# All weights ahead of the experts in 1 MB units, high and low part in one slot

## The reference, cut to what matters

```python
h = rmsnorm(x)
proj = h @ w_in + b_in                  # 1024 -> q 512, k 128, v 128, xr 1024, yr 1024, gates 2048
attn = block_attention(rope(norm(q)), rope(norm(k)), v)        # 8 query heads, 2 key heads
xc = depthwise_conv(xr)                                        # 4 taps
lru = rglru(xc, forward) + rglru(xc, backward)                 # gates, decays, scan along tokens
rec = lru * gelu(yr)
merged = sigmoid(gA) * (attn @ w_attn_o) + sigmoid(gR) * (rec @ w_lru_o)
x = x + merged @ w_out
h = rmsnorm(x)
top_val, top_idx = top_k(h @ w_router + b_router, 4)           # 32 experts
x = x + sum over the 4 experts e of gate_e * (swiglu(h @ w_gu[e] + b_gu[e]) @ w_down[e] + b_down[e])
out = rmsnorm(x) * final_g
```

## Time and profile before

| what | us |
|---|---|
| runs | 1136.24, 1137.75, 1137.98; median 1137.75 |
| span of the profiled execution, first to last instruction | 1134.2 |
| what lies around the span, against the median of the runs | 3.55 |
| TensorE busy | 1084.8 |
| VectorE busy | 371.1 |
| ScalarE busy | 237.2 |
| DMA | 439.77 MB, 388 GB/s over the span |

### The profile page before, as it was taken

One profiled execution on the slowest core, in us unless ns is written; L12 is line 12 of the kernel. 1 busy time (PEld: TensorE's weight loads), 2 busy tenths in 40 slices (PEclk: granted clock), 3 DMA queues, 4 the chain that ended last, 5 costly groups with the idle time before them and its releaser, 6 DMA issues.

```text
span 1134.2 us, 12887 instructions
## 1 busy us (share of the span) xinstructions
PE 1084.8 (96%) x5407; PEld 503.4 (44%) x5407; DVE 371.1 (33%) x645; ACT 237.2 (21%) x369; POOL 2.6 (0%) x10
## 2 busy tenths in 40 slices
PE   7999999999999999999998989898989899899987
PEld 7999899633333333333333333333333333333332
DVE  6997887522212222122121211111211212121212
ACT  5399961211111111111111110011110101010102
POOL 0000000000000000000000000000000000000000
PEclk9999999899999999999999999999999999999999
DMA  9544277999999999999999999999999999999996
GB/s 353 185 178 149 84 287 300 419 425 399 431 425 428 426 434 432 433 426 435 431 429 436 430 430 436 429 430 436 430 432 433 429 436 430 427 427 429 426 428 247
DMA packets 25637, 439.77 MB, mean 388 GB/s; under 512 B 3425, under 2 KB 4065, under 8 KB 6273
## 3 DMA queue, kind: packets, MB, share of 16 engines
q1 hardware_dynamic: 24976, 438.27, 91.5%
q10 hardware_dynamic: 624, 0.99, 0.2%
HBM read 438.20 MB, written 1.05 MB: 387 GB/s over the span
## 4 chain that ended last, share of the span: by engine, by line
PE 67%; DMA 28%; DVE 2%; SPq 1%; ACT 1%; issue 0%; DVEq 0%
PE ps L1491 26%; DMA slots<-in_w_down_dram 22%; PE ps L1500 13%; PE ps L1172 13%; DMA slots<-in_w_gu_dram 5%; PE ps L1455 5%; PE ps L1436 3%; PE ps L1549 2%; DVE slots_r L725 1%; SPq L403 1%; PE ps L1229 1%; PE ps L1450 1%; PE ps L1414 1%; PE ps L1234 0%; PE ps L1526 0%; PE ps L1274 0%
## 5 line engine op out<-in xcount | busy, mean ns | idle before, releaser
L1500 PE MATMUL ps<-slots,lru 128*64 128x512 f32 x1024 | 239.8, 610 | 17.2 <-DMA slots<-in_w_down_dram 17.2
L1491 PE MATMUL ps<-slots,lru 128*64 128x512 f32 x1024 | 227.7, 594 | 11.7 <-DMA slots<-in_w_gu_dram 11.2
L1491 PE MATMUL ps<-slots,qT 128*64 128x512 f32 x984 | 223.8, 596 | 4.6 <-DMA slots<-in_w_gu_dram 4.6
L1491 PEld LDWEIGHTS ps<-slots,lru 128*64 128x64 f32 x1024 | 74.1, 137 | 160.8 <-issue 139.7
L1491 PEld LDWEIGHTS ps<-slots,qT 128*64 128x64 f32 x984 | 68.9, 137 | 152.2 <-issue 144.8
L1500 PEld LDWEIGHTS ps<-slots,lru 128*64 128x64 f32 x1024 | 68.5, 139 | 142.5 <-issue 123.5
L1100 DVE COPY lru<-ps 128x512 f32<-128x512 f32 x32 | 22.1, 692 | 322.9 <-PE ps L1491 322.9
L1172 PE MATMUL ps<-slots_r 128*128 128x256 f32 (+1 forms) x812 | 107.7, 291 | 0.2 <-DVE slots_r L725 0.2
L1172 PEld LDWEIGHTS ps<-slots_r 128*128 128x128 f32 x812 | 102.2, 191 | 5.4 <-issue 2.5
L653 ACT ACTIVATE lru<-ps 128x512 f32<-128x512 f32 x32 | 19.1, 598 | 395.3 <-PE ps L1491 395.3
L1082 DVE TENSOR_SCALAR lru<-sq,rank_col,small 128x64 f32<-128x64 f32 x64 | 17.2, 312 | 241.8 <-PE ps L1436 241.8
(11 more groups left out here) (200 smaller groups left out, 649.3 us busy)
## 6 DMA issues: line engine op xcount, KB each, us to landing
slots<-in_w_gu_dram SPq DMA_DIRECT2D x40, 4096.0 KB, 29.2
slots<-in_w_gu_dram SPq DMA_DIRECT2D x44, 2048.0 KB, 18.9
slots<-in_w_down_dram SPq DMA_DIRECT2D x20, 4096.0 KB, 28.4
slots<-in_w_down_dram SPq DMA_DIRECT2D x22, 2048.0 KB, 20.8
slots<-in_pre_dram SPq DMA_DIRECT2D x13, 2048.0 KB, 8.2
slots<-in_w_down_dram SPq DMA_DIRECT2D x8, 512.0 KB, 31.0
slots<-in_pre_dram SPq DMA_DIRECT2D x3, 1024.0 KB, 6.9
slots<-in_w_gu_dram SPq DMA_DIRECT2D x3, 1024.0 KB, 17.4
```

Of the source, the lines that this page charges most:

```text
L1491: ins = nc.tensor.matmul(ps[64 * side:64 * side + 64, 4 + b, :], xgT[i % 2][:, k, :], rows[r][:, o:o + BANK], start=(k == 0), stop=(k == K ...
L1500: ins = nc.tensor.matmul(ps[64 * side:64 * side + 64, bank, :], actT[(i - 1) % 2][:, k, :], w[:, r, side * BANK:(side + 1) * BANK], start= ...
```

## The change

All weights ahead of the experts are loaded in 29 units of 1 MB (half a chunk; k and v are one unit). A unit lies whole in the first half of a slot; its high part is written in the second half of the same slot and its low part over the whole. Units 0 to 5 take slots 5, 2, 3, 4, 0, 1, units 6 to 22 rotate through slots 5, 2, 3, 4, and later ones use slots 6 and 2 to 5. Of the input chunks a unit is 256 of 512 columns of each of the eight rows of a partition, so its source is in pieces of 1 KB; for chunks 0, 2 and 3 and the last five it is contiguous. Splits are per unit and have new places in the programs of ScalarE and VectorE. Slots 0 and 1 take the expert chunks 0 and 1 once q is done. The first half of wide takes chunk 7 instead of 3. TensorE does all eight branches, then the mix; the part of the mix that is done bank by bank has the last two blocks instead of four. The diff, cut to what is spoken of:

```diff
-        SLOT_ORDER = [2, 3, LOWS, SLOTS - 1, 0, 1, 4, 5]
-        EARLIER = [5, 0, 4, 0, 5, 0, 1, 1]
-        FREED = {2: [(branch_ps, 3)], 0: [(mixed_ps, 1)], LOWS: [(branch_ps, KD)], 4: [(mixed_ps, 2)]}
+        UNIT = CH // 2
+        UNITS = ([(c, h) for c in range(10) for h in range(1 if c == 3 else 2)]
+                 + [(10, 0), (10, 1), (11, 0), (11, 1), (13, 0), (13, 1), (12, 0), (12, 1), (14, 0), (14, 1)])
+        Q_UNIT, KV_UNIT, BR_UNIT, MIX_UNIT = 4, 6, 19, 25
+        UNIT_SLOT = [5, 2, 3, 4, 0, 1] + [2 + (u + 1) % 4 for u in range(6, 23)] + [LOWS, 2, 3, 4, 5, LOWS]
+        UNIT_FREED = {6: (group_done, 4), 7: (group_done, 4), 8: (group_done, 6), 9: (group_done, 8), 10: (qkv_done, 4),
+                      **{u: (group_done, 2 * u - 12) for u in range(11, 23)},
+                      23: (gate_ps, 32), 24: (branch_ps, 2), 25: (branch_ps, 3), 26: (branch_ps, 4), 27: (branch_ps, 6),
+                      28: (branch_ps, 7)}
+        SLOT_ORDER = [0, 1, 2, 3, 4, 5, LOWS, SLOTS - 1]
+        FREED = {0: (qkv_done, 2), 2: (branch_ps, KD), 3: (mixed_ps, 1), 4: (mixed_ps, 2), 5: (mixed_ps, 3),
+                 LOWS: (mixed_ps, 4)}
...
-        CAST_V = (5, 9)
+        CAST_V = (9, 10, 17, 18)
+        def unit_src(u):
+            c, h = UNITS[u]
+            if c in IN_CHUNK[1:]:
+                return pre[c].rearrange("p (k n) -> p k n", k=KD)[:, :, h * TOK:(h + 1) * TOK]
+            return pre[c, :, h * UNIT:(h + 1) * UNIT]
+        def unit_low(u):
+            return ring_r[UNIT_SLOT[u]][:, 0:UNIT]
+        def unit_high(u):
+            return ring_r[UNIT_SLOT[u]][:, UNIT:]
...
+            for u in range(4):
+                unit_load(u)
...
+            sp.dma_start(ring[LOWS][:, KD * TOK:], w_lru[0]).then_inc(lruw_in, 16)
+            for u in range(6, 11):
+                unit_load(u)
+            for k in range(2):
+                expert_load(k)
+            sp.wait_ge(gate_ps, 16)
+            sp.dma_start(ring[LOWS][:, KD * TOK:], w_lru[1]).then_inc(lruw_in, 16)
+            for u in range(11, 22):
+                unit_load(u)
+            sp.wait_ge(rec_ok, 2)
+            sp.wait_ge(pv_ps, NQ // 2)
             sp.dma_start(late[:, :], expert_src(n, j)).then_inc(extra_full[0], 16)
+            half_load(extra_rows(1, 0), EXTRA[1], 0, extra_full[1])
+            unit_load(22)
+            unit_load(23)
+            half_load(wide[:, 0:2048], 7, 0, slot_full[SLOTS - 1])
+            for u in range(24, 29):
+                unit_load(u)
+            expert_load(2)
+            half_load(wide[:, 2048:], 7, 1, slot_full[SLOTS - 1])
             sp.wait_ge(merged_ok, KD)
             half_load(extra_rows(1, 1), EXTRA[1], 1, extra_full[1])
+            for k in range(3, SLOTS - 1):
                 expert_load(k)
...
@@ ScalarE
-            split_high(4)
+            split_high(7)
+            split_high(8)
             lru_gates(0, range(4))
             act.wait_ge(qk_inv, 1)
             nc.scalar.activation(qk_rstd, qk_rstd, ACT.Sqrt).then_inc(qk_rs, 1)
-            split_high(6)
             for i in range(8, 14):
                 group(i)
                 if i == 9:
                     lru_decay(0, 0)
+                    split_high(11)
                 if i == 11:
                     lru_decay(0, 1)
                     lru_decay(0, 2)
             copy_qk()
             lru_root(0)
+            split_high(12)
             for i in range(14, 16):
                 group(i)
...
-            split_high(7)
+            split_high(13)
...
             lru_gates(1, [0])
-            split_high(8, [0])
+            split_high(14)
             pair_exps(0)
             lru_gates(1, [1])
             group_pair(16)
-            split_high(8, [1])
+            split_high(15)
...
             group_pair(18)
+            split_high(16)
             lru_decay(1, 0)
...
@@ VectorE
-            split_high(5)
-            split_low(5)
+            for u in (9, 10):
+                split_high(u)
+                split_low(u)
...
             lru_input(0)
-            split_low(6)
+            split_low(11)
             lru_square(0)
             lru_scaled(0)
+            split_low(12)
             lru_scan(0)
             lru_sum(0)
...
             lru_input(1)
-            split_high(9)
-            split_low(9)
+            split_low(16)
+            split_high(17)
+            split_low(17)
             pair_max(2)
...
             pair_attn(1)
+            split_high(18)
+            split_low(18)
             pair_max(3)
...
-            split_low(10)
+            split_low(19)
+            split_low(20)
             recurrent_low(1)
             attention_low()
-            split_low(11)
+            split_low(21)
             for g in range(KD):
...
-                if g == 1:
-                    split_low(12)
-                if g == 3:
-                    split_low(13)
-                if g == KD - 1:
-                    split_low_by_halves(14)
+                if g != 3:
+                    split_low(22 + g if g < 3 else 21 + g)
...
@@ TensorE
-            for g in range(4):
+            for g in range(KD):
                 branches(g)
-            mix(0)
-            for g in range(4, KD):
-                branches(g)
-            for c in range(1, 4):
+            for c in range(ENDS):
                 mix(c)
```

More of the change, by code:

```diff
@@ L513, in _ @@
             act.dma_start(sq[:, 1:, :], squares[:, 1:, :]).then_inc(sq_in, 16)
-            split_high(0)
-            split_high(1)
+            for u in range(4):
+                split_high(u)
             act.wait_ge(lam_e, 1)
@@ L753, in _ @@
             low_part(hT_lo, hT, hT_hi).then_inc(h_lo, 1)
-            split_low(0)
-            split_low(1)
+            for u in range(4):
+                split_low(u)
             dve.wait_ge(lam_e, 2)
@@ L1174, in product, with unit @@
                 return ins
-            def chunk(c, k):
-                return [b.rearrange("p (k n) -> p k n", k=k) for b in (high(c), low(c))]
+            def unit(u, k):
+                return [b.rearrange("p (k n) -> p k n", k=k) for b in (unit_high(u), unit_low(u))]
             def transposes(rows, tp0):
@@ L1202, in first_groups @@
             def first_groups():
-                w = chunk(0, KD)
+                w = [unit(u, 4) for u in range(2)]
                 for q, (a, b, ks) in enumerate(((0, 0, range(4)), (0, 0, range(4, KD)), (0, 1, range(KD)), (1, 0, range(KD)))):
                     if q < 2:
-                        pe.wait_ge(split_hi, q + 1)
+                        pe.wait_ge(*unit_high_ok(q))
                         pe.wait_ge(h_hi, q + 1)
@@ L1239, in _ @@
             for part in range(2):
-                chunk_in(Q_CHUNK + part)
-                w = chunk(Q_CHUNK + part, KD)
-                n_col = QW if part == 0 else 2 * KVW
+                pe.wait_ge(*unit_low_ok((Q_UNIT + 1, KV_UNIT)[part]))
+                w = [unit(Q_UNIT, 4), unit(Q_UNIT + 1, 4)] if part == 0 else [unit(KV_UNIT, KD)]
+                per, n_col = (4, QW) if part == 0 else (KD, 2 * KVW)
                 for t in range(T):
@@ L1245, in _ @@
                     product(ps[:, 2 * t + part, 0:n_col],
-                            [((hT_hi[:, k, toks], hT_lo[:, k, toks]), [b[:, k, :] for b in w]) for k in range(KD)]
+                            [((hT_hi[:, k, toks], hT_lo[:, k, toks]), [b[:, k % per, :] for b in w[k // per]])
+                             for k in range(KD)]
                             ).then_inc(qkv_done, 1)
@@ L1314, in _ @@
                     values(VALUES_AT.index(i))
-            BLOCKS = CH // P
-            w_br = [chunk(c, BLOCKS) for c in BR_CHUNK]
+            BLOCKS = UNIT // P
+            w_br = [unit(u, BLOCKS) for u in range(BR_UNIT, MIX_UNIT)]
             def branches(g):
                 first = 12 * g
-                for i, c in enumerate(BR_CHUNK[:2]):
-                    if g > 0 and first <= BLOCKS * i < first + 12:
-                        chunk_in(c)
                 if g >= 2:
@@ L1358, in mix @@
                     ins = mix_bank(n, c)
[L1359 removed]
+                if c % 2 == 1:
                     ins.then_inc(mixed_ps, 1)
             def mix_end(n):
[L1363 removed]
+                if n == 0:
+                    pe.wait_ge(*unit_low_ok(MIX_UNIT + 3))
+                for c in range(ENDS, KD):
                     pe.wait_ge(merged_ok, c + 1)
```

213 lines of the change are left out of this document (85 added, 128 removed).

## The result

The change makes the kernel slower: 1147.39 us (median of 4 runs, 1144.91 to 1148.17) against 1136.99 us of the kernel before on the same chip (4 runs, 1135.75 to 1137.98), a ratio of 1.0089 with a 95% interval of 1.0074 to 1.0104. That is 10.4 us more; the prediction had 6.0 more. Its time of 1143.8 us missed by 3.6. The measured time lies inside the stated range of 1139.5 to 1148.5, but 0.4 us outside the forecast's own 1140.5 to 1147, where the rival of the choked queue begins.

What follows compares the result with a forecast made beforehand. The prediction took TensorE's arrival at the experts as the bound. Terms of 3.8 + 1.7 + 0 + 0.5 = 6.0 us took the span from 1134.2 to 1140.2 and, with 3.55 us around it, the time to 1143.8 us; range 1139.5 to 1148.5.

Steps and rivals of the forecast that it cites:

- the choked queue: Rival, 11%: loads in 1 KB pieces run at half rate, 3 to 8 us more, 1147 to 1152 us.
- The bound: Expert stage: the end is fixed by when TensorE gets to the experts, about 226 us; DMA already has lead.
- The rival in which the lead counts: Rival, 5%: the end goes by bytes landed, so earlier expert loads make it 5.1 us faster, 1132.6 us.
- the signs named: Two gate-block stops of about 2 us, half clock near 108 us, first expert matmul near 232 us, DMA idle before.
- Steps 1 to 5: First half's gates: ScalarE idles 3.3 us, waits 0.4 us for unit 11; VectorE's sum 3.9 us later; gate reads at 99.5 us.
- Step 2: DMA queue: unit 11 lands at 75.2 us behind the expert chunks, with 0.5 us for 1 KB pieces of units 10 and 11.
- Steps 6 and 7: TensorE's gate blocks stop 1.8 and 2.3 us, 3.8 us late with the start included; half clock after the second costs 1.7 us.
- the first stop: TensorE's gate block of 98.81 us waits for ScalarE's gate reads until 100.4 us, a stop of 1.8 us.
- Step 8: Attention: the cast of unit 16 moves, second decays begin 5.9 us later; cost to TensorE 0, up to 0.7 us.
- Step 9: Branches: unit 22 lands at 161.5 us, fourth branch stops 1.0 us instead of 0.56; 0.5 us more.
- Step 10: The mix: its last part does two instead of four blocks per bank; no cost.
- The sum around the span: Final total: 6.0 us added to the profiled span, plus 3.55 us taken to lie around it, gives 1143.8 us.

Runs made afterwards that it cites:

- the repaired one: Changed kernel with expert chunks 0 and 1 behind unit 14, unit 12 split early by VectorE, unit 14 cast before the gate reads, units 22 to 24 first: 1139.38 us.

## Why the prediction came out as it did

**The bound** was read rightly: the start of the experts decides. It moved by 10.0 us and the medians by 10.4, the pure delay of 4.3 us passed to the end, and 8 us more lead of the initial set were worth nothing. The rival in which the lead counts would have been faster than before, and the pair with the chunks after unit 13 and behind unit 26 speaks against it as well. Of the signs named, the first expert matmul was late (236.24 us, 232 foretold) with the end, DMA moved 137 GB/s from 234 to 236 us and 4 GB/s in the 2 us behind, and TensorE never waited for DMA in the expert stage; but the gate blocks stopped once and not twice, and the half clock stood at 101 and not near 108 us.

**Steps 1 to 5** named the right chain and mis-sized one link. ScalarE idled 3.38 us (3.3 predicted). Unit 11 landed at 76.74 us, not 75.2, and ScalarE waited 2.36 us for it, not 0.4. Step 2 had the pieces at 0.5 us for units 10 and 11 together. From issue to landing unit 11 took 8.6 us, in the layout by unit 7.3: the pieces cost 1.3. The other 0.7 of the 2.0 beyond 74.7 us lies in the step's chain of landings: the two expert chunks ahead landed 11.1 us behind unit 10 where the step had 9.8 (11.0 also in the layout by unit), while unit 10 was issued at 54.34 us and not at 55. The scaling began at 90.72 instead of 88.8 us, the low part took its 2.28 (2.3 predicted), the gate reads started at 101.18 instead of 99.5 and 108.05 instead of 106.4.

**Steps 6 and 7** came to nearly the right sum by a wrong course, and in that was luck: 5.5 us predicted up to the second gate block, 6.1 measured. The step that failed is the first stop, 1.8 us. It became 3.76, since the reads were 1.7 us later, and the half clock followed it and not the second: 1.2 GHz from 101.0 us for 6.8 us. The slower stretch took the time that the second stop would have stood. ScalarE's second set of reads began here, with no idle time before it:

```profile
108.05 1.58 ACT L480 ACTIVATE lru<-ps,cst 128x256 f32<-128x256 f32 x4
```

By the prediction's own step the second gate block could start two reads later, at 108.85 us. At full clock TensorE would have been there 4.60 us after 102.17, at 106.77, and would have stopped for 2.1 us (in the run with the chunks after unit 13 it was 2.04). It started at 109.54. So of the 2.77 us behind the first stop about 2.1 stand in for the second stop and 0.7 are the clock's own cost, an estimate from these rows, where the sum had 1.7. Two errors partly cancelled: the reads came 1.7 us later than the steps had them, and the clock cost 1.0 us less than the sum had for it. The rows of a 1.8 us stop were no measure for a stop of 3.8.

Halving the transfers cost little rate. While a 2 MB chunk and four loads of 1 MB queued behind each other, the kernel after moved this:

```profile
160.00:174.00 14.00, 12.71 (x106) 12.51 (x105) 8.13 (x11) 6.10 (x7) 0.00 (x0) 1.00 1.00 421
```

That is 421 GB/s, 2% below the 431 of the 2 MB chunks. The Trainium skill, page "DMA: Bandwidth & Descriptors", section "Bandwidth", gives 341 GB/s for 1 MB, in a table of loads issued from GpSimd. The trace does not agree with it for loads that SP issues and that queue. Unit 11, in pieces of 1 KB, landed 2.65 us behind the load ahead of it, where the prediction's estimate from that figure was 3.1.

**Step 8** held: -0.07 us between the second gate blocks and the branches, with TensorE never stopped there.

**Step 9** failed most: 0.5 us predicted, 4.0 measured. Its places were right, 6.1 us shifted: unit 21 issued at 152.83 (152.8), the late chunk at 154.18 (154.7). But the landings came 5.42 and 3.45 us apart for the late chunk and the half chunk, where the step had 4.9 and 2.5. Unit 22 landed at 169.49 us, 1.9 later than the shifted 167.6. The rows are unit 22's issue (it is the first of two), its time to landing, and VectorE's wait for the cast ahead of its low part:

```profile
159.79 0.82 SPq L323 DMA_DIRECT2D slots<-in_pre_dram  x2
...
slots<-in_pre_dram SPq DMA_DIRECT2D x1, 1024.0 KB, 9.7
...
171.45 2.29 DVE L735 TENSOR_TENSOR slots_r<-slots,slots_r 128x2048 fp32r<-128x2048 f32 x1 [5.33 <-ACT slots_r L448]
```

Cast, low part and merge took what the step gave them, and a stop of 1.0 became one of 2.99. The sum had no term for the clock here; 3.4 us at half rate added 1.58. That the chain hangs on the queue there is shown by units 22 and 23 going first (0.94 us, clock kept). Why the two loads took 1.5 us more than back to back is not settled; DMA moved 287 GB/s from 155 to 156 us and 413 from 157 to 167.

**Step 10** held: -0.04 us. **The sum around the span** read its 3.55 us wrongly: only 1.8 lie around a span, the rest was the distance of that one execution from the median. The forecast does not suffer by it, since it is the median of 1137.75 plus 6.0. But that median fell to 1136.99 with the fourth run, and this 0.8 us makes the miss look smaller: the change itself was foretold 4.4 us too small.

Of the rivals, the choked queue lies nearest in time (1147 to 1152), but it had the pieces cost 3 to 8 us, and without them the experts start 1.7 us earlier. The forecast's mechanism is what happened, with two terms too small, unit 11's landing in step 2 (0.5 us with its pieces, 2.0 measured) and the branches in step 9, and with the place of the half clock wrong.

## What to carry to other kernels

When one wait is lengthened by two causes in a row, price the stop at the far end of its uncertainty, and the clock with it: the stop that was 1.3 us without the late unit and 3.8 us with it had 6.8 us of half clock beside it. A load's place in a fixed queue is a cost to whatever stands behind it, even while DMA is half idle; put transfers that nobody needs soon behind the ones that an engine waits for. A repair that the medians of a few runs do not show may still be seen in a place of the trace: the layout by unit brought the experts forward by 1.7 us in the kernel after and by 1.8 us in the repaired one, but only eleven runs of each resolved it in the time.

## What the runs showed of the hardware

- Loads in 1 KB pieces held up the issuing queue here. Near the start SP's next issue behind such a unit took 4.64 us; with contiguous units it took 0.44. The first rows are the kernel after, the second the layout by unit:

```profile
7.06 4.64 SPq L346 DMA_DIRECT2D pbuf<-in_rows_dram  x1
```

```profile
3.70 0.44 SPq L342 DMA_DIRECT2D pbuf<-in_rows_dram  x1
```

- TensorE's stop of 3.76 us, and one of 3.39 in the run with units 22 and 23 first, each went with 6.8 us at a clock of about 0.5. Stops of 2.03 us had 3.4 us of it in two runs and none in a third (2.04 us), with the same blocks around them. In the branches stops of 2.54, 2.56, 2.91 and 2.99 us each had 3.4 us of it, and one of 2.84 in the run with the early low part none. So from 2 to 3 us the clock could not be told from the stop alone. Single stops of 0.94 to 1.46 us had none.
- The chunk that the prediction looked at (issued about 41 us after the first expert matmul, with little else on the queue) took 8.5 to 11.2 us to land over the twelve traces, for the same 2 MB. In the first 60 us or so of the expert stage, once its loads follow each other, single gaps between landings of up to 7.6 us stand among those of 4.9.
